# Opening of a two-layer DiT kernel: modulation products on four column strips, tokens loaded first, last four groups between the chunks of the first two weight tiles

## The reference, cut to what matters

```
mod   = jax.nn.silu(c) @ w_mod[l] + b_mod[l]          # (1, 6*1024): sh1, sc1, gt1, sh2, sc2, gt2
mod_c = jax.nn.silu(c_ctx) @ w_mod[l] + b_mod[l]
h  = modulate(rms_norm(x,  g_norm1[l]), sh1,  sc1)    # x * rsqrt(mean x^2) * g * (1 + sc1) + sh1
hc = modulate(rms_norm(xc, g_norm1[l]), csh1, csc1)
gq, gk, gv, dq, dk, dv, cu = project_heads(h @ w_in[l], ...)
```

## Time and profile before

| | |
|---|---|
| median of 3 runs | 2379.27 us (2377.58 to 2379.94) |
| the profiled execution | 2377.62 us |
| its span | 2375.8 us |
| PE busy | 2302.5 us, 97% of the span |
| DVE, ACT, POOL busy | 57%, 43%, 36% |
| first matmul of the program | 10.48 us |
| first matmul of the pair of tiles | 48.56 us |
| first matmul behind the pair | 66.86 us |

### The profile page before, as it was taken

One profiled execution on the slowest core, in us unless ns is written; L12 is line 12 of the kernel. 1 busy time (PEld: TensorE's weight loads), 2 busy tenths in 40 slices (PEclk: granted clock), 3 DMA queues, 4 the chain that ended last, 5 costly groups with the idle time before them and its releaser, 6 DMA issues.

```text
span 2375.8 us, 32833 instructions
## 1 busy us (share of the span) xinstructions
PE 2302.5 (97%) x12832; PEld 2073.7 (87%) x12832; DVE 1359.5 (57%) x2068; ACT 1018.6 (43%) x1991; POOL 854.8 (36%) x593
## 2 busy tenths in 40 slices
PE   7999999999999989999999999999999999999999
PEld 4888899999999989999999997778878877888887
DVE  5566677699976745654443347667889845111111
ACT  4666676652252342212212237667654254322222
POOL 2566312100034424453333335752220243544443
PEclk9999999999999999999999999999999999999999
DMA  6101111123224523434343431111103323333333
GB/s 260 46 19 36 37 36 36 32 85 94 67 71 138 173 70 112 137 108 133 116 141 97 126 98 54 32 41 45 54 27 103 106 94 106 104 98 95 98 94 97
DMA packets 134665, 208.96 MB, mean 88 GB/s; under 512 B 12528, under 2 KB 66032, under 8 KB 134384
## 3 DMA queue, kind: packets, MB, share of 16 engines
q1 hardware_dynamic: 134512, 206.86, 27.5%
HBM read 202.62 MB, written 4.19 MB: 87 GB/s over the span
## 4 chain that ended last, share of the span: by engine, by line
PE 80%; DVE 11%; ACT 3%; issue 2%; DMA 1%; SPq 1%; POOL 1%; DVEq 0%; ACTq 0%
PE acc L717 21%; PE acc L719 21%; PE acc L718 21%; DVE X L1841 4%; PE sco L916 3%; PE aux L717 3%; PE aux L719 3%; PE aux L718 3%; PE aux L929 2%; PE acc L951 2%; DVE NM L1753 1%; DVE RB L1707 1%; PE aux L894 1%; DVE M L1707 1%; DVE WLO L1707 1%
## 5 line engine op out<-in xcount | busy, mean ns | idle before, releaser
L610 POOL TENSOR_TENSOR WLO<-STG,WHI 128x512 fp32r<-128x512 f32 (+2 forms) x500 | 691.8, 1404 | 1407.3 <-ACT WHI L1177 1242.3
L717 PE MATMUL acc<-H,WHI 128*128 128x384 f32 (+2 forms) x1976 | 711.6, 360 | 16.9 <-DVE H L2006 8.3
L719 PE MATMUL acc<-H,WLO 128*128 128x384 f32 (+2 forms) x1976 | 694.5, 351 | 0.0
L718 PE MATMUL acc<-H,WHI 128*128 128x384 f32 (+2 forms) x1976 | 693.9, 351 | 0.0
L1177 ACT ACTIVATE WHI<-STG 128x512 fp32r<-128x512 f32 (+2 forms) x616 | 331.0, 586 | 395.6 <-PE acc L719 354.0
L717 PEld LDWEIGHTS acc<-H,WHI 128*128 128x128 f32 x1976 | 373.2, 189 | 46.3 <-issue 16.7
L719 PEld LDWEIGHTS acc<-H,WLO 128*128 128x128 f32 x1976 | 372.8, 189 | 25.5
L718 PEld LDWEIGHTS acc<-H,WHI 128*128 128x128 f32 x1976 | 373.6, 189 | 24.1 <-issue 0.2
L717 PE MATMUL acc<-RB,WHI 128*128 128x384 f32 (+1 forms) x816 | 288.6, 354 | 3.2 <-DVE RB L1707 1.4
L719 PE MATMUL acc<-RB,WLO 128*128 128x384 f32 (+1 forms) x816 | 287.6, 352 | 0.0
L718 PE MATMUL acc<-RB,WHI 128*128 128x384 f32 (+1 forms) x816 | 287.5, 352 | 0.0
(11 more groups left out here) (160 smaller groups left out, 2830.1 us busy)
## 6 DMA issues: line engine op xcount, KB each, us to landing
STG<-in_w_fi SPq DMA_DIRECT2D x176, 256.0 KB, 2.7
M<-in_w_mod SPq DMA_DIRECT2D x56, 512.0 KB, 4.6
STG<-in_w_in SPq DMA_DIRECT2D x104, 256.0 KB, 2.6
STG<-in_w_gate SPq DMA_DIRECT2D x96, 256.0 KB, 2.7
STG<-in_w_fo SPq DMA_DIRECT2D x64, 256.0 KB, 2.7
STG<-in_w_br SPq DMA_DIRECT2D x96, 128.0 KB, 2.1
FIRST<-in_w_mod SPq DMA_DIRECT2D x8, 1024.0 KB, 20.2
SOONB<-in_w_mod SPq DMA_DIRECT2D x16, 512.0 KB, 4.2
```

Source lines behind the costliest of these rows:

```text
L610: nc.gpsimd.tensor_tensor(WLO[:, s, a:a + w], STG[:, g, a:a + w], WHI[:, s, a:a + w].bitcast(F32), ALU.subtract).then_inc(S("w_split"), 1)
L717: nc.tensor.matmul(dst, lh, rh, start=first, stop=False)
L718: nc.tensor.matmul(dst, lh, rl, start=False, stop=False)
L719: return nc.tensor.matmul(dst, ll, rh, start=False, stop=last)
```

## The change

- `first_rows` (L1043 before, L1056 after): the weights are now 128 x 32 (the two columns of silu and 30 of zeros, in a new view SCW, which lies in the place of the cosine table K until that is loaded), and chunk k writes the 32 PSUM partitions from 32*(k % 4) on: four column strips of the array, each with two chunks accumulated. The four partial sums stand on partitions 0, 32, 64 and 96 (1, 33, ... for the context). ScalarE copies 128 x 256 in place of 2 x 256.
- `first_turn`: in place of a transpose, a matmul with the copied rows as weights (128 x 128) and a selector SEL (128 x 2, ones at the right partitions) as moving operand, which adds the four strips and turns them in one. SEL is one small reduction on VectorE.
- SyncE: the tokens X now go first, in two halves with a semaphore each, then groups 0 and 1, weight tiles 0 and 2, groups 2 to 7, tile 1, and then, behind a new wait until all eight row products are done (`f_full`), the angles and the taps, which overwrite SCW.
- ScalarE: the squares come before the first two rows, the split of tile 0 before the root, that of tile 2 behind the first chunk of H; `first_row(2)` to `(7)` stand one before each of the first six chunks.
- VectorE: two of the four sums and one gain move behind the first two chunks.
- TensorE: groups 0 and 1, norm sums, turns 0 and 1, groups 2 and 3, their turns, then the pair. Groups 4 and 5 run between its chunks 0 and 1, their turns between 1 and 2, groups 6 and 7 between 2 and 3, their turns between 3 and 4.
- FIRST lies 32 KB per partition further on, so that the groups still in use are not under the part of H that is written.

Names in the order below: sco0 and sco1 are PSUM buffers of rows and turned columns, G is FROW, K is the buffer of constants (SCW in it), RLN is the buffer that holds SEL, acc and aux are the accumulators.

```diff
@@ -206,7 +206,8 @@
 
 
 
-        with nc.sbuf_tensor("FIRST", [P, 2 * MOD_FIRST, KC * P], F32) as FIRST:
+        with nc.sbuf_tensor("UNDERF", [P, 4 * KC * TOK - 2 * MOD_FIRST * KC * P], F32), \
+                nc.sbuf_tensor("FIRST", [P, 2 * MOD_FIRST, KC * P], F32) as FIRST:
             pass
         with nc.sbuf_tensor("UNDER", [P, 2 * KC * TOK], F32), nc.sbuf_tensor("SOONB", [P, 2 * KC * TOK], F32) as SOONB:
             pass
@@ -269,7 +270,9 @@
         XS = M[:, 6 * TOK:8 * TOK].rearrange("p (n t) -> p n t", n=2)
         OSQ, ORS = T[:, 512:768], T[:, 0:512].rearrange("p (n q) -> p n q", n=2)
         MROW = [R[0:4, 64 + MOD_GROUP * i:64 + MOD_GROUP * (i + 1)] for i in range(2)]
-        FROW = [G[0:2, 16 + 256 * i:16 + 256 * (i + 1)] for i in range(2)]
+        FROW = [G[:, 256 * i:256 * (i + 1)] for i in range(2)]
+        SCW = v4(K, K_COS, KC, 32)
+        SEL = RLN[:, 0:2]
 
         first = [g for i in range(MOD_FIRST // 2) for g in (i, i + MOD_FIRST // 2)]
         LAMS = U[:, 0:VECS - V_LAM]
@@ -534,19 +537,24 @@
             sp.dma_start(V[:, :], vecs[:, 0:V_LAM]).then_inc(S("vecs"), 16)
             sp.dma_start(LAMS, vecs[:, V_LAM:VECS]).then_inc(S("lams"), 16)
             sp.dma_start(K[:, K_ONES:CONSTS], consts[:, K_ONES:CONSTS]).then_inc(S("consts"), 16)
+            for i in range(2):
+                sp.dma_start(X[:, 4 * i:4 * i + 4, :], xT[:, 4 * i:4 * i + 4, :]).then_inc(S(f"x{i}"), 16)
             first_groups(0)
-            sp.dma_start(X[:, :, :], xT).then_inc(S("x"), 16)
+            tile(w_in[0, 0], KC * P)
+            tile(w_in[0, 2], KC * P)
             for i in range(1, MOD_FIRST // 2):
                 first_groups(i)
             mods = 2 * MOD_FIRST
             for l in range(DEPTH):
-                for t in [0, 2, 1, 3, *range(4, 10)]:
+                for t in [0, 2, 1, 3, *range(4, 10)][2 if l == 0 else 0:]:
                     tile(w_in[l, t], KC * P)
                     if l and t == 3:
 
                         sp.wait_ge(S("x_done"), l)
                         sp.dma_start(x_next, X[:, :, 0:LAT]).then_inc(S("saved"), 16)
-                    if l == 0 and t == 2:
+                    if l == 0 and t == 1:
+
+                        sp.wait_ge(S("f_full"), MOD_FIRST)
                         sp.dma_start(K[:, 0:K_ONES], consts[:, 0:K_ONES]).then_inc(S("angles"), 16)
                         sp.dma_start(WDW[:, :, :, 0:TAPS], wdw).then_inc(S("wdw"), 16)
                 for h in range(4):
@@ -637,6 +645,7 @@
             nc.gpsimd.memset(EC[:, 1:2], HEAD * EPS).then_inc(S("ec"), 1)
             nc.gpsimd.memset(EC[:, 2:3], 0.0).then_inc(S("ec"), 1)
             nc.gpsimd.memset(WDW[:, :, :, TAPS:4 * TAPS4], 0.0).then_inc(S("wdw_zero"), 1)
+            nc.gpsimd.memset(SCW, 0.0).then_inc(S("scw_zero"), 1)
             nc.gpsimd.memset(SCX[:, :].bitcast(F32), 0.0).then_inc(S("scx_zero"), 1)
             nc.gpsimd.memset(MOD[:, 1, :, :, :], 0.0).then_inc(S("mod_zero"), 1)
             nc.gpsimd.memset(T[:, :], 0.0).then_inc(S("t_zero"), 1)
@@ -747,13 +756,15 @@
                 tile_end.append(("aux_full", c.at("aux")) if gate else ("acc_full", c.at("acc") + 1))
                 c.step("tile")
 
-            def tile_pair(rngs, others, ready, name, other, sem="h_ready", lag=0):
+            def tile_pair(rngs, others, ready, name, other, sem="h_ready", lag=0, ahead={}):
 
 
                 t = c.at("tile")
                 dsts = [open_acc() for _ in rngs]
                 odsts = [open_aux(n) for n in range(len(others))]
                 for step in range(KC + lag):
+                    for run, group in ahead.get(step, ()):
+                        run(group)
                     for n, k in enumerate((step, step - lag)):
                         if not 0 <= k < KC:
                             continue
@@ -1040,9 +1051,11 @@
                 if n >= 2:
                     pe.wait_ge(S("f_row"), n - 1)
                 for k in range(KC):
-                    mm = nc.tensor.matmul(sco[0][0:2, 512 * (n % 2):512 * (n % 2) + MOD_GROUP], SC[:, k, :],
+
+                    q = slice(32 * (k % 4), 32 * (k % 4) + 32)
+                    mm = nc.tensor.matmul(sco[0][q, 512 * (n % 2):512 * (n % 2) + MOD_GROUP], SCW[:, k, :],
                                           FIRST[:, 2 * n + k // 4, k % 4 * MOD_GROUP:(k % 4 + 1) * MOD_GROUP],
-                                          start=k == 0, stop=k == KC - 1)
+                                          start=k < 4, stop=k >= 4)
                 mm.then_inc(S("f_full"), 1)
 
             def first_turn(n):
@@ -1050,20 +1063,22 @@
                 if n >= 2:
                     pe.wait_ge(S("f_sum"), n - 1)
                 for k in range(2):
-                    t = nc.tensor.transpose(sco[1][:, 512 * (n % 2) + 2 * k:512 * (n % 2) + 2 * k + 2],
-                                            FROW[n % 2][:, k * P:(k + 1) * P], IDENT[0:2, 0:2])
-                t.then_inc(S("f_turned"), 1)
-
-            pe.wait_ge(S("silu_c"), 1)
-
-            for n in range(MOD_FIRST):
+                    mm = nc.tensor.matmul(sco[1][:, 512 * (n % 2) + 2 * k:512 * (n % 2) + 2 * k + 2],
+                                          FROW[n % 2][:, k * P:(k + 1) * P], SEL, start=True, stop=True)
+                mm.then_inc(S("f_turned"), 1)
+
+            pe.wait_ge(S("scw"), 1)
+            first_rows(0)
+            first_rows(1)
+            pe.wait_ge(S("consts"), 16)
+            norm(0, 0, TOK)
+            pe.wait_ge(S("sel"), 1)
+            first_turn(0)
+            first_turn(1)
+            for n in (2, 3):
                 first_rows(n)
-                if n == 1:
-                    pe.wait_ge(S("consts"), 16)
-                if n == 3:
-                    norm(0, 0, TOK)
-                for m in {1: (0, 1), 3: (2, 3), 6: (4, 5), 7: (6, 7)}.get(n, ()):
-                    first_turn(m)
+            for n in (2, 3):
+                first_turn(n)
             pe.wait_ge(S("scx"), 1)
             for l in range(DEPTH):
                 if l:
@@ -1075,7 +1090,9 @@
                 n = n_tok(l)
                 uses = lambda t, rngs: [at[(l, 0, t), r] for r in range(len(rngs))]
                 if paired(l, 0):
-                    tile_pair(wide, slim, 2 * KC * l, (l, 0, "k"), (l, 0, "q"))
+                    tile_pair(wide, slim, 2 * KC * l, (l, 0, "k"), (l, 0, "q"),
+                              ahead={1: [(first_rows, 4), (first_rows, 5)], 2: [(first_turn, 4), (first_turn, 5)],
+                                     3: [(first_rows, 6), (first_rows, 7)], 4: [(first_turn, 6), (first_turn, 7)]} if l == 0 else {})
                     tile(KC, normed, wide, name=(l, 0, "v"), where=(0, KC // 2),
                          between=lambda: head_sums(1, TOK, (l, 0, "ks"), uses("k", wide)))
                     head_sums(0, n, (l, 0, "qs"), uses("q", slim), "aux")
@@ -1492,11 +1509,11 @@
                 if (l, k) == (0, 0):
                     norm_root(n)
                     for j in range(KC):
-                        if j in (1, 3):
+                        if j < 6:
+                            first_row(j + 2)
+                        gained_hi(l, k, j, n)
+                        if j == 0:
                             hi()
-                        for r in {2: (4,), 3: (5,), 4: (6,), 5: (7,)}.get(j, ()):
-                            first_row(r)
-                        gained_hi(l, k, j, n)
                     return
                 gained_hi(l, k, 0, n)
                 for j in range(1, KC):
@@ -1522,6 +1539,8 @@
             act.sem_inc(S("mod_turned"), 1)
             fn(SC[:, :, :], v4(V, V_C, KC, 2), ACT.Silu, sem="silu_c")
             act.wait_ge(S("silu_c"), 1)
+            act.wait_ge(S("scw_zero"), 1)
+            fn(SCW[:, :, 0:2], SC[:, :, :], ACT.Copy, sem="scw")
             act.wait_ge(S("scx_zero"), 1)
             fn(SCX4[:, :, 0:2], SC[:, :, :], ACT.Copy, sem="scx_hi")
             exp_set()
@@ -1533,15 +1552,15 @@
                 act.wait_ge(S("f_full"), n + 1)
                 if n >= 2:
                     act.wait_ge(S("f_turned"), n - 1)
-                fn(FROW[n % 2], sco[0][0:2, 512 * (n % 2):512 * (n % 2) + MOD_GROUP], ACT.Copy, sem="f_row")
-
+                fn(FROW[n % 2], sco[0][:, 512 * (n % 2):512 * (n % 2) + MOD_GROUP], ACT.Copy, sem="f_row")
+
+            for j in range(KC):
+                if j % 4 == 0:
+                    act.wait_ge(S(f"x{j // 4}"), 16)
+                fn(MM[:, j, :], X[:, j, :], ACT.Square, sem="nsq")
             first_row(0)
             first_row(1)
-            act.wait_ge(S("x"), 16)
-            for j in range(KC):
-                fn(MM[:, j, :], X[:, j, :], ACT.Square, sem="nsq")
-            first_row(2)
-            first_row(3)
+            hi()
             for l in range(DEPTH):
                 wide, slim = ranges(l, True), ranges(l, False)
                 n = n_tok(l)
@@ -2031,7 +2050,7 @@
 
                 if (l, k) == (0, 0):
```

(10 more changed lines are left out.)

## The result

The changed kernel takes 2366.18 us (median of 4 runs, 2364.23 to 2366.99), the kernel before 2378.43 (4 runs, 2377.18 to 2379.94): ratio 0.9947 with the 95% interval 0.9930 to 0.9964, so 12.3 us faster. Forecast were 2372.5 us, 6.8 us faster. The direction came true, and the amount was nearly twice as large. The first rival, full overlap of the strips (2367.8 us), is near what was measured.

The account below looks back on a forecast made before the run. TensorE, busy 97% of the span, bounds the kernel: pair start 31.7 plus 28.35 us ends at 60.05, not 66.86, gaining 6.8 us; 2379.27 - 6.8 = 2372.5 us, range 2366 to 2384.

Parts of the forecast that it names:

- The first rival, full overlap of the strips: Group products on TensorE: strips overlap fully, 0.88 us a group (1.4 allowed), gain 10.6 to 12.4, time 2367.8 us; chance 0.25.
- the disputed price: a group of 8 products: Group products on four strips: passes start in program order, 9 passes, 2.0 us a group, between bounds 0.88 and 3.54.
- the four groups of the pair: Groups 4 to 7, run on TensorE inside the pair of tiles: four at 2.0 us, 8.0 us together.
- The start: TensorE's first matmul of the pair of tiles: to come at 31.7 us, not 48.56.
- Four turns: Turns of groups 4 to 7 on TensorE inside the pair: 0.2 us each, 0.8 us together.
- the switches: Changes between array shapes on TensorE inside the pair: some six at 0.2 us, 1.2 us together.
- The low spell: One more spell of TensorE at the low clock (1.2 GHz) inside the pair, as before: 1.7 us.
- TensorE sets the end of the pair: End of the pair: VectorE's last chunk comes at 56.6 us, before TensorE's last step at 57.9; TensorE barely sets the end.
- The landing rule: Load queue: a load lands once 1.0 to 1.2 MB more than its own place has moved; 1.05 taken.
- The taps do not come late: Taps loaded behind the wait for all products: nothing taken; the bound was landing at 62.3 us, 1.4 us late.
- No overlap: Rival on the group products: 3.54 us a group, pair ends at 71.2, 4.3 us slower, 2383.6 us; chance 0.16.
- The clock stays low: Rival on TensorE's early rows and groups at 1.2 GHz: pair ends at 64 to 65, gain 2, 2377 us; chance 0.14.

Follow-up runs that it names:

- Experiment 3: Changed kernel with neighbouring chunks on the same strip (chunk k to strip k // 2, not k % 4): 2364.44 us, ratio 0.9937 to the kernel before.
- experiment 12: Changed kernel with the same 128 x 32 weights, but all eight chunks on one strip: 2383.41 us, ratio 1.0014 to the kernel before.
- experiment 11: The changed kernel run again unaltered, for comparison and a second profile: 2365.46 us, ratio 0.9942 to the kernel before.
- Experiment 5: Changed kernel with the token halves loaded behind groups 0 and 1, not ahead: 2370.30 us, ratio 0.9955 to the kernel before.
- experiment 1: Changed kernel's new order and loads with the old products, row copies and turns: 2381.38 us, ratio 1.0011 to the kernel before.
- experiment 2: Kernel before in its old order, with products on four strips and selector turns: 2379.71 us, ratio 1.0002 to the kernel before.
- experiment 10: Old order with strips, plus filler matmuls in TensorE's waits before the pair: 2379.06 us, ratio 1.0003 to the kernel before.
- experiment 4: Changed kernel with groups 4 to 7 and their turns in front of the pair: 2370.48 us, ratio 0.9963 to the kernel before.

## Why the prediction was wrong

**The step that failed is "the disputed price: a group of 8 products", 9 passes and 2.0 us.** It assumed that passes start in program order and that a second pass behind its own first one holds back the next chunk. Measured: 0.93 us, the time of 4 passes (4 x 0.221 = 0.88). Experiment 3 shows that it is not luck of the order, experiment 12 that it is the strips. I gave the row of the scores the right reading (parts of the array work side by side), and then let an untested rule on two passes take half of it away again.

In the numbers: the four groups of the pair were to cost 8.0 us and cost 4.2 (2.36 and 1.86 for two each, the first partly at the low clock). That is 3.8 us. The start was to be 31.7 and was 30.6, 1.1 us earlier: shorter groups, and loads that came 1.0 to 1.4 us before the rule's moments, less the slow pace, which was reckoned for group 0 alone and lasted until about 28 us. Four turns and the switches were to cost 2.0 and cost 2.0, but by luck: two sizes were wrong and cancel. A turn by the selector costs 0.4 us and not 0.2, the price of a transpose of 2 partitions (the two double turns take 0.81 each up to the next matmul), so four cost 1.6 in place of 0.8; the switches cost 0.4 in place of 1.2 (the four re-entries into the pair 0.1 each beyond 0.1735). The low spell was 1.7 and is 1.5 to 1.6. 60.05 - 3.8 - 1.1 - 0.15 = 55.0, and 54.95 was measured.

The Trainium skill, TensorEngine Tiling ("Theoretical Speedup"), gives up to 4x for a small dimension of 32; the traces agree, 3.54 / 0.93 = 3.8, in f32 with two passes. The Trainium skill, TensorE: Matmul & The Clock Gate, Part 3 ("The mechanism"), says that matmuls start and end in strict order; experiment 3 cannot say whether they do, but it shows that no such order costs anything here.

**Steps that held.** TensorE sets the end of the pair, barely, as was said: VectorE's last chunk is ready at 52.43 and needed at 52.87 (56.6 and 57.9 said). The landing rule: token halves 9.94 and 13.97 (11.3 and 15.1 said), groups 0 and 1 16.70 and 19.18 (17.7 and 20.2 said), so about 1 us pessimistic, and 17.36 and 19.84 in experiment 11. Squares, additions, row copies of 128 partitions (0.38 us against 0.37) and SEL are hidden. The taps do not come late: the queue is empty by then, and the angles in front of them land in 4.0 us. Experiment 5 shows the norm chain hidden only because the tokens are loaded first: behind groups 0 and 1 they start the pair 5.5 us later.

**The rivals.** *No overlap* was to end at 71.2 and lose 4.3 us; experiment 12 built just that, ends at 69.7 and loses 3.1, experiment 1 loses 2.3. Its working was sound: the pair starts at 36.05 (36.7 said) and takes 33.6 us (34.5 said), as no low spell falls in it (1.00 from 36 to 70 us). *The clock stays low* came in part: the pace is low up to 28 us, which costs the start about 1.3 us by the two profiles of this kernel (experiment 11), and once inside the pair; but it did not cost the gain. *Full overlap* was given 54.5 to 56.3 and 2367.8 us: the end, 54.95, lies within, and 2366.18 was measured. Its chance of 0.25 was too small for a case that had a measured row behind it, while the forecast's 2.0 had none.

**Where the gain comes from.** Order alone: +2.3 us. Strips alone: no change clear of noise. Both: -12.3. By the traces, the ScalarE and VectorE chain behind weight tile 0 holds the pair in the old order (experiments 2 and 10), so shorter products only give idle time. The new order takes that chain away and makes TensorE the bound of the opening; then each microsecond of a group counts. By experiments 4 and 5, the place of the groups inside the pair brings about 4 us (the clock's part in it not separated), and the tokens in front 2 to 4.

**What stays open.** In the profiled executions the gain is 11.9 us at 76 us of the span and 10.6 at the end. The medians say 12.3, and single runs of one kernel differ by 3 us, so no cause was sought. Why the low spell in the pair comes in some executions of one order and not in others was not settled either.

## What to carry to other kernels

Before shortening an engine's work, look at what it waits for behind that work: strips alone gained nothing here, and the order alone lost. Products with few weight columns belong on separate column strips (here at about a quarter of the time), and a selector matmul can add and turn the strips in one. Where a price has no row, and the nearest row shows a mechanism at work, give the forecast to that row and leave the self-made rule as the rival.
